# One 512-column product under held weights in the first halves of two MLPs

## What is computed

```python
def sq_relu_mlp(u, w1, w2):
    return jnp.square(jax.nn.relu(u @ w1)) @ w2
...
        h = h + rms_norm(mix, norm_post_mix[l])
        m = sq_relu_mlp(rms_norm(h, norm_pre_mlp[l]), mlp_w1[l], mlp_w2[l])
        h = h + rms_norm(m, norm_post_mlp[l])
```

## Time and profile before

| what | value |
|---|---|
| median of 3 runs | 2654.67 us (2654.6 to 2656.53) |
| span of the profiled execution, first to last instruction | 2654.2 us |
| PE busy | 2578.9 us (97%) |
| DVE busy | 1805.5 us (68%) |
| ACT busy | 1203.1 us (45%) |
| share of PE in the chain that ended last | 92% |
| mean granted TensorE clock | 0.988 |

### The profile page before, as it was taken

The page is one execution under the profiler, slowest core; times in us unless marked ns, Lnnn a source line. Parts: engine busy times, 40 slices in busy tenths (PEclk is TensorE's granted clock), DMA queues, the critical chain, the costliest instruction groups (busy, mean ns, idle before and its releaser), DMA issues.

```text
span 2654.2 us, 44813 instructions
## 1 busy us (share of the span) xinstructions
PE 2578.9 (97%) x16616; PEld 2338.9 (88%) x16616; DVE 1805.5 (68%) x2617; ACT 1203.1 (45%) x1589; POOL 138.4 (5%) x261
## 2 busy tenths in 40 slices
PE   6999999999999999999999899999899999999997
PEld 6889988998889898989898888988689999999996
DVE  3777777776876656565656867767876666666666
ACT  3555445544554434343434644444453434343433
POOL 2220222012100000000000000000000000000000
PEclk8999999999999999999999999999999999999999
DMA  8665566556446666566666555555356665666664
GB/s 182 199 189 176 172 192 196 166 181 190 160 141 193 190 190 190 190 190 189 190 189 191 175 167 166 158 175 167 120 169 196 185 194 186 193 186 194 187 193 135
DMA packets 267175, 477.17 MB, mean 180 GB/s; under 512 B 16577, under 2 KB 50210, under 8 KB 265298
## 3 DMA queue, kind: packets, MB, share of 16 engines
q1 hardware_dynamic: 263296, 457.76, 55.7%
q0 software_dynamic: 3296, 18.12, 2.8%
q10 hardware_dynamic: 498, 0.18, 0.0%
HBM read 470.70 MB, written 5.31 MB: 179 GB/s over the span
## 4 chain that ended last, share of the span: by engine, by line
PE 92%; DVE 4%; ACT 2%; issue 1%; DMA 1%; POOL 0%; ACTq 0%; DVEq 0%; POOLq 0%; SPq 0%
PE ps L1241 29%; PE ps L1242 29%; PE ps L1243 29%; PE ps L1387 1%; ACT whl L562 1%; DVE whl L820 1%; ACT junk L565 1%; PE ps L1406 0%; DVE h L929 0%; DVE xhl L890 0%; DMA par_rows<-a_conv_b 0%; PE ps L1466 0%; DVE stat L842 0%; PE ps L1380 0%; PE ps L1390 0%
## 5 line engine op out<-in xcount | busy, mean ns | idle before, releaser
L820 DVE TENSOR_TENSOR whl<-raw,whl 128x1024 fp32r<-128x1024 f32 x865 | 1069.8, 1237 | 771.3 <-ACT whl L562 761.9
L562 ACT ACTIVATE whl<-raw 128x1024 fp32r<-128x1024 f32 x865 | 916.2, 1059 | 1280.6 <-PE ps L1243 1253.9
L1241 PE MATMUL ps<-xhl,whl 128*128 128x256 f32 x3072 | 866.0, 282 | 6.3 <-DVE xhl L890 6.3
L1242 PE MATMUL ps<-xhl,whl 128*128 128x256 f32 x3072 | 859.2, 280 | 0.0
L1243 PE MATMUL ps<-xhl,whl 128*128 128x256 f32 x3072 | 858.7, 280 | 0.0
L1241 PEld LDWEIGHTS ps<-xhl,whl 128*128 128x128 f32 x3072 | 580.1, 189 | 11.4 <-DVE xhl L890 7.7
L1242 PEld LDWEIGHTS ps<-xhl,whl 128*128 128x128 f32 x3072 | 580.2, 189 | 2.9 <-issue 1.7
L1243 PEld LDWEIGHTS ps<-xhl,whl 128*128 128x128 f32 x3072 | 580.0, 189 | 0.0
L1241 PE MATMUL ps<-whl,bhl 128*128 128x512 f32 x1408 | 552.0, 392 | 4.7 <-DVE bhl L951 3.6
L1242 PE MATMUL ps<-whl,bhl 128*128 128x512 f32 x1408 | 550.5, 391 | 0.0
L1243 PE MATMUL ps<-whl,bhl 128*128 128x512 f32 x1408 | 549.9, 391 | 0.0
(11 more groups left out here) (194 smaller groups left out, 1877.6 us busy)
## 6 DMA issues: line engine op xcount, KB each, us to landing
raw<-mlp_w SPq DMA_DIRECT2D x512, 512.0 KB, 4.1
raw<-a_in_proj SPq DMA_DIRECT2D x161, 512.0 KB, 4.5
raw<-a_out_proj SPq DMA_DIRECT2D x64, 512.0 KB, 4.5
raw<-b_w_q SPq DMA_DIRECT2D x32, 512.0 KB, 3.7
raw<-w_k SPq DMA_DIRECT2D x32, 512.0 KB, 3.7
raw<-w_v SPq DMA_DIRECT2D x32, 512.0 KB, 3.7
raw<-b_out_proj SPq DMA_DIRECT2D x32, 512.0 KB, 3.7
cumb<-cum_scratch POOLq DMA_DIRECT2D x8, 1024.0 KB, 7.7
```

The lines of the kernel that those rows point to most:

```text
L562: sc.activation(whi[:, s.split, :], raw[:, s.raw, :], ACT.Copy).then_inc(hi_ready, 1)
L820: ve.tensor_tensor(out=wlo[:, s.split, :], in0=raw[:, s.raw, :], in1=whi[:, s.split, :].bitcast(F32), op=ALU.subtract).then_inc(lo_ready, 1)
L1241: te.matmul(outs, lh, rh, start=start, stop=False, skip_group_check=True)
L1242: te.matmul(outs, lh, rl, start=False, stop=False, skip_group_check=True)
```

## The change

In the 15 ups of each MLP behind the first, the high half of w1 is loaded as weights once and streams a row of 512 columns, x's high and low halves side by side; the low half of w1 then streams the 256 columns of x's high half. Each feature tile takes a whole bank, so an up takes banks 0 to 3, always the same, and acc takes 4 to 7. The bank's second half is the high-by-low product: ACT copies it out (`ulow`), and DVE adds it to the first half ahead of the old scale and clip, which is now one instruction of 1024. The first up of each MLP stays with three matmuls, in banks 6 and 7. `xhl` is laid out so that the two halves of a row are neighbours; its size and its start stay.

```diff
+MLP_TURN_BANKS = (4, 5, 0, 1, 2, 3, 4, 5)
+RS_BANK = {1: 4, 2: 2, 3: 4}
...
+    def out_bank(ph):
+        return MLP_OUT_BANK if ph in (mlp0, mlp1) else 3
...
-    UP_BANKS = ((0, 1), (2, 7))
+    FIRST_UP_BANKS, UP_BANK, MLP_OUT_BANK = (6, 7), 0, 4
...
+            n = KT * 2 * S
+            room = stack.enter_context(nc.sbuf_tensor(name, [P, n + phase // 4], F32R, align_bytes=UNIT))
+            both = room[:, phase // 4:phase // 4 + n].rearrange("p (k n) -> p k n", k=KT)
+            return both[:, :, 0:S], both[:, :, S:], both
...
                 def up(which, b):
-                    act.wait_ge(u_ready, 2 * (8 * (r - 1) + b + 1))
+                    if above(b):
+                        sc.activation(ulow[:, :, :], ps[:, UP_BANK:UP_BANK + 4, S:], ACT.Copy).then_inc(u_low, 1)
+                    act.wait_ge(u_ready, 8 * (r - 1) + b + 1)
...
                 def up(which, b):
-                    for n in range(2):
-                        ve.scalar_tensor_tensor(out=relu[:, n, :].rearrange("p (f s) -> p f s", f=2),
-                                                in0=ps[:, UP_BANKS[which][n], :].rearrange("p (f s) -> p f s", f=2), scalar=0.0,
-                                                in1=rs_row[:, :].unsqueeze(1).to_broadcast([P, 2, S]),
-                                                op0=ALU.max, op1=ALU.mult).then_inc(u_ready, 1)
+                    features = relu[:, :, :].rearrange("p n (f s) -> p (n f) s", f=2)
+                    if above(b):
+                        dve.wait_ge(u_low, 15 * ((r - 1) // 2) + b)
+                        link(ve.tensor_tensor(out=features, in0=ps[:, UP_BANK:UP_BANK + 4, 0:S], in1=ulow[:, :, :], op=ALU.add))
+                        sums = features
+                    else:
+                        sums = ps[:, FIRST_UP_BANKS[0]:FIRST_UP_BANKS[1] + 1, :].rearrange("p n (f s) -> p (n f) s", f=2)
+                    ve.scalar_tensor_tensor(out=features, in0=sums, scalar=0.0,
+                                            in1=rs_row[:, :].unsqueeze(1).to_broadcast([P, 4, S]),
+                                            op0=ALU.max, op1=ALU.mult).then_inc(u_ready, 1)
...
+            def feature_major_once(s, i, x):
+
+                pe.wait_ge(lo_ready, s.n + 1)
+                wh, wl = slot(s, 2)
+                for f in range(BLK // P):
+                    for j in range(2):
+                        k = 2 * i + j
+                        c = slice(f * P, (f + 1) * P)
+                        te.matmul(ps[:, UP_BANK + f, :], wh[:, j, c], x[2][:, k, :], start=k == 0, stop=False,
+                                  skip_group_check=True)
+                        last = te.matmul(ps[:, UP_BANK + f, 0:S], wl[:, j, c], x[0][:, k, :], start=False,
+                                         stop=k == KT - 1, skip_group_check=True)
+                last.then_inc(slab_used, 1)
...
-                    if i == 0 and above(b, 1):
-                        pe.wait_ge(b_hi, ph.features(b - 2))
-                    feature_major(s, i, UP_BANKS[which], x)
+                    if not above(b):
+                        feature_major(s, i, FIRST_UP_BANKS, x)
+                        return
+                    if i == 0 and above(b, 1):
+                        pe.wait_ge(u_ready, 8 * (r - 1) + b)
+                    feature_major_once(s, i, x)
```

More of the change, by code:

```diff
@@ L64, with turn_bank @@
 TURN_BANKS = (3, 4, 5, 6, 2, 7, 3, 4)
+MLP_TURN_BANKS = (4, 5, 0, 1, 2, 3, 4, 5)
+RS_BANK = {1: 4, 2: 2, 3: 4}
+def turn_bank(r, i):
+    return (MLP_TURN_BANKS if r in (1, 3) else TURN_BANKS)[i]
 H_PIECES = ((0, 256), (256, 512), (512, 1024), (1024, 1536), (1536, 2048))
@@ L220, in halves, with pairs @@
                     for i in range(2)]
+        def pairs(name, phase, stack=ctx):
+            n = KT * 2 * S
+            room = stack.enter_context(nc.sbuf_tensor(name, [P, n + phase // 4], F32R, align_bytes=UNIT))
+            both = room[:, phase // 4:phase // 4 + n].rearrange("p (k n) -> p k n", k=KT)
+            return both[:, :, 0:S], both[:, :, S:], both
         def sem(name):
@@ L228, in build @@
         whi, wlo = halves("whl", [P, LEAD, SLAB], 0)
-        xhi, xlo = halves("xhl", [P, KT, S], X_PHASE)
+        xhi, xlo, xboth = pairs("xhl", X_PHASE)
         b0 = halves("bhl0", [P, 4, S], B_PHASE[0])
@@ L285, in build @@
         sq = mb("sq", [P, MT, BLK])
+        ulow = mb("ulow", [P, 4, S])
         b1 = halves("bhl1", [P, 4, S], B_PHASE[1], mem)
@@ L321, in build @@
         xt_done, x_hi, x_lo = sem("xt_done"), sem("x_hi"), sem("x_lo")
-        b_hi, h_ready, u_ready = sem("b_hi"), sem("h_ready"), sem("u_ready")
+        b_hi, h_ready, u_ready, u_low = sem("b_hi"), sem("h_ready"), sem("u_ready"), sem("u_low")
         xk_hi, xk_lo, rs_spread, rs_row_ready = sem("xk_hi"), sem("xk_lo"), sem("rs_spread"), sem("rs_row_ready")
@@ L586, in x_halves @@
                     act.wait_ge(xt_done, KT // 2 * r + i + 1)
[L587 removed]
+                    x_half(i, turn_bank(r, i), xhi, col, x_hi)
             def spread_rs(r):
                 act.wait_ge(rs_spread, r)
[L592 removed]
+                sc.activation(rs_row[:, :], ps[:, RS_BANK[r], 0:S], ACT.Copy).then_inc(rs_row_ready, 1)
             def output_norm(ph, r, i):
@@ L916, in last_output @@
                     cols = y[:, t, (NT - 1) * BLK:]
-                    ve.tensor_tensor(out=cols, in0=cols, in1=ps[:, 5 + t, :], op=ALU.add).then_inc(done, 1)
+                    ve.tensor_tensor(out=cols, in0=cols, in1=ps[:, out_bank(ph) + 2 + t, :], op=ALU.add).then_inc(done, 1)
             def weigh_early(r, i):
@@ L1137, in mlp @@
                 with dve.Fori(0, 7) as t:
-                    chain.enter(t, 4)
+                    chain.enter(t, 6)
                     steps(ph, 8, MLP_BODY, lambda u, i: step(u, i, 2 * t), t, 32)
-                chain.leave(7, 4)
+                chain.leave(7, 6)
                 steps(ph, 232, MLP_LAST, lambda u, i: last_output(ph, i) if u == "acc1" else step(u, i, 14), urgent=True,
@@ L1285, in output @@
                     pe.wait_ge(acc_added, a - 1)
-                token_major(s, i % 2, 2, 3 + 2 * (nt % 2), (bhi[which], blo[which]))
+                token_major(s, i % 2, 2, out_bank(ph) + 2 * (nt % 2), (bhi[which], blo[which]))
             def transpose_scaled_x():
@@ L1308, in transpose_x @@
                         k = 2 * i + j
-                        last = te.transpose(ps[:, TURN_BANKS[i], j * S + t * P:j * S + (t + 1) * P], h[:, t, k * P:(k + 1) * P],
+                        last = te.transpose(ps[:, turn_bank(r, i), j * S + t * P:j * S + (t + 1) * P], h[:, t, k * P:(k + 1) * P],
                                             ident[:, :])
```

18 lines of the change are left out of this document (9 added, 9 removed).

## The result

The change made the kernel slower: 2682.86 us (median of 4 runs, 2679.36 to 2683.87) against 2655.41 (4 runs, 2654.6 to 2656.53). The ratio is 1.0101, with a 95% interval of 1.0088 to 1.0115. The forecast was 2659.4 and its range ended at 2673, so both were too low: the profiled span grew from 2654.2 to 2680.0 us, by 25.8, where 4.7 were forecast.

A forecast was written before the change was run, and what follows sets the result against it. It took PE's stream of matmuls to bound the MLPs. From a span of 2654.2 us, 24.0 of stalls added and 19.3 from joining removed gave 2658.9, so a median of 2659.4 us, range 2646 to 2673.

The forecast's parts named there:

- it is one for each matmul, not one for each column, and where the tiles start moves it: MLP ups: a matmul's surplus over its columns is fixed, so the long row takes 223.3 ns; 19.3 us less in all.
- stays at 116.7: MLP ups: the remaining matmul of 256 columns in a product keeps its time of 116.7 ns.
- joining gives back little: Rival, ups: the long row takes 226.9 ns (2666.1 us) or twice 116.7 (2678.7 us); chance 0.27.
- at nothing ... an acc of 21.8 us lies between: Ups' single set of banks: waiting for u_ready of the up before costs nothing, as leaving takes some 5 us.
- if two ups stood side by side, this would cost about 5 us each: Ups' single set of banks: without an acc between two ups, the wait for u_ready would cost about 5 us each.
- The stall: PE ahead of slab 4 of each acc waits for DVE's late add to y: 0.8 us a block, 24.0 us in all.
- The ACT copy: ACT's 1.02 us copy from PSUM lies beside DVE's split and costs nothing, with 0.25 us to spare.

The follow-up runs named there:

- the first experiment: The changed kernel, but PE's wait ahead of an up is on a new semaphore with one early count, so the loop's first up doesn't wait: 2673.36 us.
- the second experiment: The changed kernel, but behind an up DVE makes its first add to y ahead of its split of slab k + 6: 2657.76 us.
- the last experiment: The changed kernel with the free first up and the early add to y, and the low half of whl alone moved 32 bytes: 2674.25 us, one run.
- the fastest version: The changed kernel with both edits, the first up not waiting and DVE's first add to y ahead of its split: 2646.01 us, 0.9962 of before.

## Why the prediction was wrong

**The step that failed first: "it is one for each matmul, not one for each column, and where the tiles start moves it".** It rested on two rows (13.2 for 256 columns of `khl`, 13.6 for 512 of `whl` past `bhl`), and from it came 223.3 ns for the long row, a product of 340.0 and a gain of 19.3 us. Measured are 228.6 and 118.3 (the short one, "stays at 116.7", moved too), a product of 347.0 and a gain of (350.2 - 347.0) x 1920 = 6.1 us. The agreement of the two rows was chance: it compared streams of different tiles against different weights. With the very same tiles at the same starts a 256 has a surplus of 13.2 and a 512 one of 23.0. The rival *joining gives back little* was the right one in size, given 0.27; its own figures (226.9, or twice 116.7) lie on both sides of the 228.6. Its mechanism, a surplus that goes with the columns, isn't shown either: with `xhl` at 16 the long row's is 12.0 and the short one's 14.8. The Trainium skill's fixed part of 2.5 ns ("TensorE: Matmul & The Clock Gate", Back-to-back issue gap) gave a gain of 4.8 us, and I had set it aside because its distances don't fit; the distances are off here, the difference nearly right. The term was too large by 13.2 us.

**The step that failed second: "at nothing ... an acc of 21.8 us lies between".** It is so 28 times in 30. The same sentence went on "if two ups stood side by side, this would cost about 5 us each", and they do, once at the head of each MLP; the front part of this document even says so ("Up 0 stands ahead of the loop"), and the instruction that waits stands in the order shown. The price came out near: 9.5 us for two by the medians of the first experiment, some 11 by the starts in the trace after. That was partly luck, since the 5 us were meant as waiting alone; measured are 3.3 us of waiting and some 2.4 of low clock, which the prediction didn't have. The count was wrong, and no rival covered it.

**The stall: right.** The mechanism, its place and its size: 1.18 us later, from two instructions of 1024 columns each where two of 512 stood, `sq` 2.52 behind the add's start for 2.50, PE 0.23 behind DVE's end for 0.25, 0.77 to 0.91 us a block for 0.8 (0.85 on average by the accs), 25.1 us in all by the second experiment for 24.0. The ACT copy is hidden with 0.23 us to spare, for 0.25.

**The sum.** To the span of 2658.9 that was forecast, add 13.2 for the joined row, about 11 for the two first ups and 1.6 for the stalls, and take off 4.9 for the start and the attention together. That is 2679.8, where 2680.0 was measured. The last of these the rows of before didn't give: it is PE's 2.84 us wait for `nmax` and the low clock behind it, which the kernel after lacks though its code there is the same.

**What stays open.** What held DVE 2.3 us longer ahead of `nmax` in the attention of before; and there is one trace of each kernel, so how often it does isn't known. And what makes the surplus of a matmul: relative starts (a long row from 225.3 to 236.3 ns), order (228.6 or 233.8) and the start of a neighbour's tile (an acc's from 227 to 233.2) all count, but neither of the two mechanisms tried explains the last experiment.

## What to carry to other kernels

When a buffer goes from two sets to one, walk through the order of the work at both ends of the loop, not just its steady state: here the condition on the loop's register couldn't leave out the first trip, and there the wait was for something that has nothing to do with the buffer; a semaphore of its own with one early count gave 9.5 us back. When work is added ahead of an engine's queue, ask which instruction behind it someone waits for, and whether that one can be moved ahead of one that nobody wants yet; here a swap of two instructions gave back 25 us. Take a matmul's cost from a stream with the same tiles in the same places and order, and where there is none, keep the whole distance between the nearest rows as the range, for a surplus that agrees in two unlike streams may do so by chance. And compare phases, not only medians: of the 9.8 us by which the fastest version beats the kernel before, a third lies in a phase whose code is the same.

## What the hardware showed unexpectedly

- With everything else the same, a product of 768 columns takes 346.7 to 353.1 ns at six starts of `xhl` against the others, and moving all tiles together from 0 to 32 bytes changes nothing (353.1 both times).
- Long rows among themselves take 233.8 ns, and between short ones 228.6.
- A gap of 3.02 us on PE is followed by a clock of 0.50, and the up behind it takes 2.4 us longer; without the gap the clock stays at 1.00.
- At the same place of the attention, with the same code, a gap of 2.84 us on PE came with a clock of 0.51 over the next 6 us in one program, and a gap of 0.56 us with 1.00 in another.
